# Expert gather of a two-layer diffusion backbone: groups of four slots in place of two, in the same ring of eight

## What is computed

```python
def peer(h, wq, keys, u_tab, v_tab):      # cut: N tokens, 8 heads, top 16 experts of each head
    q = (x @ wq).reshape(N, PEER_HEADS, 2, PEER_DKEY // 2)
    s = jnp.einsum('nhpd,hpkd->nhpk', q, keys)
    top_s, top_i = lax.top_k(s, K)
    ...
    def block(args):
        xb, eb, gb = args
        a = jax.nn.gelu(jnp.einsum('tkd,td->tk', u_tab[eb], xb), approximate=False)
        return jnp.einsum('tk,tkd->td', gb * a, v_tab[eb])
```

## Time and profile before

| | |
|---|---|
| time, median of 3 runs (lowest to highest) | 6070.39 us (6068.23 to 6082.94) |
| the profiled execution's own time | 6077.12 us |
| its span, first to last instruction | 6075.3 us |
| mean granted TensorE clock | 0.815 |
| busy: PE, VectorE, ScalarE, GpSimd | 4146.3, 2900.3, 1672.5, 1468.7 us |
| indirect gathers | 1342.26 MB, 55.1% of the 16 DMA engines over the span |
| other DMA | 361.79 MB, 16.2% |

### The profile page before, as it was taken

The page is one execution under the profiler, slowest core; times in us unless marked ns, Lnnn a source line. Parts: engine busy times, 40 slices in busy tenths (PEclk is TensorE's granted clock), DMA queues, the critical chain, the costliest instruction groups (busy, mean ns, idle before and its releaser), DMA issues.

```text
span 6075.3 us, 63558 instructions
## 1 busy us (share of the span) xinstructions
PE 4146.3 (68%) x22120; PEld 2508.5 (41%) x22120; DVE 2900.3 (48%) x6824; ACT 1672.5 (28%) x4712; POOL 1468.7 (24%) x1295
## 2 busy tenths in 40 slices
PE   3779668879894587547566666778847765556554
PEld 0567545556563344224223334567744432211111
DVE  1221657644446544664545443522184446754544
ACT  0210126333342343223322222310114422222222
POOL 0000012212221133223344341000003332335444
PEclk7769879968997798778788888957978877777777
DMA  8214448747895599679999995102439998889998
GB/s 337 93 52 140 169 169 306 291 164 274 312 381 228 204 410 398 264 280 367 366 401 418 392 421 206 42 1 100 159 124 388 420 370 320 331 338 421 410 415 363
DMA packets 258449, 1708.10 MB, mean 281 GB/s; under 512 B 37616, under 2 KB 39120, under 8 KB 71248
## 3 DMA queue, kind: packets, MB, share of 16 engines
q0 software_dynamic: 184320, 1342.26, 55.1%
q1 hardware_dynamic: 73808, 361.79, 16.2%
HBM read 1685.91 MB, written 17.92 MB: 280 GB/s over the span
## 4 chain that ended last, share of the span: by engine, by line
PE 42%; DMA 24%; DVE 14%; ACT 5%; issue 5%; DVEq 3%; POOL 3%; ACTq 2%; SPq 1%; PEld 0%; PEldq 0%; POOLq 0%
PE psum L398 25%; DMA arena<-in_uv,arena 21%; PE psum L722 10%; POOL arena L1026 3%; DVE arena L1858 3%; DVE arena L1775 1%; DVE arena L1768 1%; DVE arena L1769 1%; DMA arena<-in_w_ada 1%; PE psum L359 1%; PE psum L568 1%; PE psum L569 1%; ACT arena L1335 1%; ACT arena L1122 1%; DVE arena L1772 1%
## 5 line engine op out<-in xcount | busy, mean ns | idle before, releaser
L1026 POOL DMA_INDIRECT arena<-in_uv,arena x1280 | 1464.8, 1144 | 4571.3 <-PE psum L722 2919.2
L722 PE MATMUL psum<-arena 64*64 64x512 f32 x10240 | 1579.8, 748 | 1180.5 <-ACTq L1336 1101.5
L1858 DVE CUSTOM_DVE_ANT_0 arena<-arena 128x1024 f32<-128x1024 f32 x1280 | 1555.3, 1226 | 1412.1 <-DMA arena<-in_uv,arena 1359.2
L398 PE MATMUL psum<-arena 128*128 128x256 f32 x8352 | 1934.2, 391 | 101.2 <-DVEq L1355 80.1
L398 PEld LDWEIGHTS psum<-arena 128*128 128x128 f32 x8352 | 1604.4, 194 | 537.7 <-issue 174.8
L722 PEld LDWEIGHTS psum<-arena 64*64 64x64 f32 x10240 | 394.2, 158 | 2183.1 <-ACTq L1336 1502.1
L1329 ACT ACTIVATE arena<-arena 128x2 f32<-128x2 f32 x640 | 130.9, 204 | 1559.2 <-DVEq L1860 1543.2
L1335 ACT ACTIVATE arena<-arena 128x64 f32<-128x64 f32 x1280 | 375.9, 340 | 45.2 <-issue 1.0
L359 PE MATMUL psum<-arena 128*128 128x128 f32 (+1 forms) x680 | 131.0, 350 | 362.9 <-DVE arena L1410 115.0
L1332 ACT ACTIVATE arena<-arena 128x1 f32<-128x1 f32 x1280 | 307.4, 287 | 46.2 <-issue 2.4
L359 PEld LDWEIGHTS psum<-arena 128*128 128x128 f32 (+1 forms) x680 | 99.9, 183 | 414.2 <-issue 216.1
(11 more groups left out here) (201 smaller groups left out, 2712.3 us busy)
## 6 DMA issues: line engine op xcount, KB each, us to landing
arena<-in_w_mix SPq DMA_DIRECT2D x120, 768.0 KB, 7.5
arena<-in_w_in SPq DMA_DIRECT2D x88, 1024.0 KB, 5.7
arena<-in_w_ada SPq DMA_DIRECT2D x32, 1536.0 KB, 17.3
arena<-in_w_wq SPq DMA_DIRECT2D x40, 1152.0 KB, 5.4
arena<-in_w_wo SPq DMA_DIRECT2D x20, 1024.0 KB, 8.8
arena<-in_uv,arena POOLq DMA_INDIRECT x1280, 11.2
arena<-ada_rows SPq DMA_DIRECT2D x15, 512.0 KB, 5.2
arena<-x_rows SPq DMA_DIRECT2D x14, 512.0 KB, 6.2
```

The lines of the kernel that those rows point to most:

```text
L398: ins = mm(out, a, b, start=(i == 0), stop=(i == last))
L722: ins = mm(psum[o, r_ * 512:r_ * 512 + 512], DIAG[rows, c, :], RING[rows, sl, D + half * 512:D + (half + 1) * 512], start=first, stop=last ...
L1026: pool.indirect_dma_start(RING[:, sl, :], None, io["uv"], bass.IndirectOffsetOnAxis(IDX[:, t, h * TOPK + k:h * TOPK + k + 1], 0)).then_inc ...
L1858: V_.tensor_tensor_reduce(out=RING[:, sl, 0:D], in0=RING[:, sl, 0:D], in1=XT[:, u % 2, :], scale=1.0, scalar=0.0, op0=ALU.mult, op1=ALU.ad ...
```

## The change

Groups have four slots, so a unit has 32 groups and two groups share the ring of eight. The lags become 0, 1 and 2: ScalarE works, in call i, the group whose dots VectorE makes in the same call, and PE the group before. The leads become six groups (24 slots), and the two points in a unit at which SyncE loads the next tokens' activations and the residual are written as shares of `GROUPS`, which leaves them where they were. Nothing else is changed; each slot has the same instructions, except that there is one gelu, and one set of waits and signals, for four slots.

```diff
 RS = 8
-GS = 2
+GS = 4
 GROUPS = PH * TOPK // GS
-LAG_ACT, LAG_PE, LAG_TAIL = 1, 2, 3
+LAG_ACT, LAG_PE, LAG_TAIL = 0, 1, 2
...
-    return [(a, [], 0), (b, p0, 0), (c1, p1[:cut], 0), (c2, p1[cut:], 8), (d, [], 0), (e1, p2[:cut], 0),
-            ([("final", 2, ())], p2[cut:cut + GROUPS], 8), ([("final", 3, ())], p2[cut + GROUPS:cut + GROUPS + 16], 8),
-            ([("final", 4, ())], p2[cut + GROUPS + 16:], 16), ([("final", 5, ())], [], 0)]
+    return [(a, [], 0), (b, p0, 0), (c1, p1[:cut], 0), (c2, p1[cut:], 6), (d, [], 0), (e1, p2[:cut], 0),
+            ([("final", 2, ())], p2[cut:cut + GROUPS], 6), ([("final", 3, ())], p2[cut + GROUPS:cut + GROUPS + 16], 6),
+            ([("final", 4, ())], p2[cut + GROUPS + 16:], 6), ([("final", 5, ())], [], 0)]
...
-                    if g == 40 and u + 1 < len(UNITS) and state["xt"] == u + 1 and (UNITS[u + 1][0], UNITS[u + 1][1] // 2) in h2_ready:
+                    if g == GROUPS * 5 // 8 and u + 1 < len(UNITS) and state["xt"] == u + 1 and (UNITS[u + 1][0], UNITS[u + 1][1] // 2) in h2_ready:
...
-                    if g == 16:
+                    if g == GROUPS // 4:
```

## The result

The changed kernel takes 6627.05 us (median of 4 runs, 6619.59 to 6629.79) against 6070.22 us (median of 4 runs of the kernel before); the ratio is 1.0911, 95% interval 1.0892 to 1.0929. The profiled execution has a span of 6628.0 us. The forecast was 6563 us, range 6290 to 6800. The ratios further down are each against runs of the kernel before made beside the run in question.

The account below looks back on a forecast made before the run. Dense work bounds b and gathers at full DMA rate bound c2 and units 8 and 9; two groups lift the ring's loop above DMA time. Segment terms 161 + 136 + 40 + 86 + 25 + 25 + 20 = +493 gave 6563 us, range 6290 to 6800.

Parts of the forecast that it names:

- The loop: Ring of two groups of four, PE done to PE done: 25.5 us for eight slots, 408 us a unit.
- quick landing: Rival: four gathers landed after 13.0 us, loop 23.3 us, total 6406 us; chance 0.15.
- cold PE: Rival: all PE bursts at 1.2 GHz (7.4 us) and ScalarE's wait holding up dense work, total 6795 us; chance 0.13.
- some +200, 6270 us: Total by the skill page's DMA fit: four gathers landed some 11.6 us after first issue, loop 21.9 us.
- Units 8 and 9: Last gather-bound units: 408 us each against 333 and 322, +161 us (bounds +59 and +229).
- c2: Units 4 and 5, same loop with weight chunks: 424 us a unit against 360 and 352, +136 us.
- Route steps of e1: Eight steps of 12 slots, third group issued only after PE's burst: 10.8 us later each, +86 us.
- c1's route steps: Eight steps of eight slots, PE gets its second half group late: 3.1 us each, +25 us.
- merge steps: Steps with 110 + 160 slots and weight chunks: 3.35 us a slot against 3.2 before, +40 us (0 to +103).
- Small stages of c1: 88 slots with tight ScalarE-VectorE chains: +25 us (0 to 50), estimated from half of the rise a slot in c2.
- b: Segment where dense work sets the pace and covers the loop: +20 us (-20 to +60).
- Faster: Rival: DMA queue never runs dry; route steps gain 40 us, table loads in b some 20, total 6010 us; chance 0.04.

Follow-up runs that it names:

- two_act_in_step: Kernel before, groups of two, lags 0, 2, 3: ScalarE in step with the dots, PE two groups behind as before; 6094.2 us, ratio 1.0036.
- four_freed_singly: Changed kernel, but PE signals after every slot and GpSimd waits for one slot in place of four; 6288.57 us, ratio 1.0343 against the kernel before.
- two_in_step: Kernel before with groups of two kept and only the lags changed to 0, 1, 2; 6277.73 us, ratio 1.0333.
- two_ring_six: Kernel before with groups of two, lags 0, 1, 2 and a ring of six slots in place of eight; 6589.31 us, ratio 1.0839.
- one_pe_four: Kernel before with groups of one, lags 1, 4, 5 (PE four slots behind), eight bubbles, slots freed singly; 6031.58 us, ratio 0.9924.

## Why the prediction held

**The loop.** Predicted 25.5 us, measured 24.88 (25.4 the turn before). Term by term: first issue to fourth dot 15.2, measured 16.1 and 14.5; ScalarE 2.6, measured 2.4 (dot's end 6024.54 to 6026.94); PE 6.2, measured 6.53 and 6.04. The quick landing (13.0 us) was not seen in these units (the shortest of 64 is 13.2), the cold PE at 7.4 us neither (the longest burst is 6.6). The loop as cause is shown from two sides: groups of two with the same lags in calls bring units 8 and 9 back to 330 and 323 us, and an earlier release alone recovers 21 to 46 us a unit with groups of four.

The Trainium skill (DMA: Bandwidth & Descriptors, Anatomy of one DMA — SWDGE (gpsimd) path) would put the fourth landing some 11.6 us after the first issue, an estimate; in the trace the fourth dot starts after 14.5 and 16.1 us. The prediction did well to go by its rows. Its "some +200, 6270 us" for that fit is too low by its own steps: 21.9 us a loop gives +45 in units 8 and 9, +20 in c2, +57 in the e1 route steps and +110 for the rest, +232 and 6302 us.

**Units 8 and 9:** +161 predicted, +140 measured. **c2:** +136 predicted, +135 measured.

**Route steps of e1:** +10.8 us a step predicted, (359.5 - 299.2) / 7 = 8.6 measured. Timeline of one step of the changed kernel:

```profile
5557.16 1.23 DVE L1858 CUSTOM_DVE_ANT_0 arena<-arena 128x1024 f32<-128x1024 f32 x1 [0.16 <-issue]
...
5564.24 9.16 PE L722 MATMUL psum<-arena 64*64 64x512 f32 x64 [20.18 <-ACTq L1336]
...
5570.28 0.94 POOL L1026 DMA_INDIRECT arena<-in_uv,arena  x1 [21.24 <-PE psum L722]
...
5575.89 1.23 DVE L1858 CUSTOM_DVE_ANT_0 arena<-arena 128x1024 f32<-128x1024 f32 x1 [9.23 <-DMA arena<-in_uv,arena]
...
5584.20 1.23 DVE L1858 CUSTOM_DVE_ANT_0 arena<-arena 128x1024 f32<-128x1024 f32 x1 [1.26 <-DMA arena<-in_uv,arena]
...
5590.02 0.49 DVE L1765 MAX8 arena<-arena 128x8 f32<-128x128 f32 x2 [4.59 <-ACT arena L1299]
```

The order of events is the predicted one, counted from the first dot, with the prediction in brackets: PE at +7.1 (7.5), third group issued at +13.1 (14.0), fourth dot at +27.0 (29.2), VectorE's next head at +32.9 (35.1). The mis-sized term is the landing, 13.9 us here in place of 15.2. c1's route steps: 256.6 us for seven before, 276.2 after, 2.8 us a step where 3.1 was predicted.

**Mis-sized: the merge steps.** "Merge steps ... +40", while the 24 sigmoids (L1262) of the 30 steps span 294.5 us after in c1 against 251.3, and 401.3 against 346.4 in e1: +98 already. The term that was wrong is the price of before, "I take 3.2". Windows of these steps in c1, before, after, and with four slots freed singly:

```profile
2078.00:2329.00 251.00, 208.72 (x1173) 124.13 (x1173) 115.58 (x200) 118.50 (x269) 90.84 (x78) 0.94 0.98 396
```

```profile
2108.00:2402.00 294.00, 221.82 (x1185) 130.18 (x1183) 118.00 (x206) 106.77 (x254) 85.92 (x80) 0.86 0.89 349
```

```profile
2093.00:2356.00 263.00, 213.13 (x1186) 128.41 (x1184) 117.04 (x206) 107.59 (x256) 93.61 (x80) 0.92 0.98 395
```

Before, the DMA share is 0.98: merge steps were gather-bound too, at 3.06 us a slot in c1 and 2.89 in e1, close to the 2.93 that the prediction had worked out from the transfers alone. After, they take 3.51 and 3.34, near the predicted 3.35, and a median turn of 28.2 and 27.4 us where 26.8 was predicted (PE's burst is 5.3 and 5.1 us, not the warm 3.9). So the loop was right here too; what it replaced was cheaper than assumed.

The timeline of a c1 merge step after shows two waits that the sum did not hold:

```profile
2255.31 1.23 DVE L1858 CUSTOM_DVE_ANT_0 arena<-arena 128x1024 f32<-128x1024 f32 x1 [1.80 <-DMA arena<-in_uv,arena]
...
2260.30 0.38 ACT L1262 ACTIVATE arena<-psum 128x256 f32<-128x256 f32 x1
...
2260.71 0.42 DVE L1729 TENSOR_TENSOR arena<-arena,psum 128x256 f32<-128x256 f32 x1 [4.17 <-ACT arena L1262]
...
2261.31 1.23 DVE L1858 CUSTOM_DVE_ANT_0 arena<-arena 128x1024 f32<-128x1024 f32 x1 [0.17 <-issue]
...
2265.19 10.67 PE L398 MATMUL psum<-arena 128*128 128x256 f32 x48
...
2269.59 1.06 ACT L1335 ACTIVATE arena<-arena 128x64 f32<-128x64 f32 x4
...
2275.79 3.66 PE L722 MATMUL psum<-arena 64*64 64x512 f32 x32
```

From the last dot (ends 2256.54) it is 4.8 us to the next, spent in ScalarE's group, the sigmoid's table load, the sigmoid that waited behind them, and the product that needs it. And a diagonal ready at 2270.7 waits until 2275.79, since PE is in two dense steps. It is tempting to book the loss on these waits, but other runs speak against it. VectorE's product (L1729) in all waited for the 24 sigmoids of c1, before, after, and freed singly (us, times):

```profile
  DVE arena L1729: 27.6, 11
```

```profile
  DVE arena L1729: 111.2, 24
```

```profile
  DVE arena L1729: 107.4, 23
```

With single slots released the wait is still there, yet the same 24 sigmoids span 262.7 us, and 354.8 in e1: +20 in place of +98, at a DMA share of 0.98. In two_act_in_step it is 86.1 us for a span of 257.0. The wait for PE is not longer than before either: from the last diagonal of a group to PE's burst it is 25 us in all in c1 after, 68 before. So at least four fifths of what the 24 steps lost goes through the late release of slots, that is the loop; the waits show in VectorE's idle time and cost at most the rest.

**Small stages, b.** Small stages of c1: +25 predicted; from the last index write of c1 to the closing of unit 3 it is 288.6 us before and 321.6 after, +33. b: +20 predicted, -4 by closings. The closings flatter it: the last index write of b's routing stands at 2064.9 before and 2097.5 after, so b's dense end is 33 us later, and the table books that on unit 2. No run isolates what b lost.

**The sum.** Four terms were too high, by 42 us together (units 8 and 9, c2, the route steps of e1 and of c1). The merge steps were too low by some 70: with the six steps behind the sigmoids in c1 and in e1 they lost about 111 us, over the upper bound of 103. Small stages, b and ends of segments that no term held add some 30. So the total rose by 557 us where 493 was forecast, and a part of the agreement is luck: errors of both signs cancel. The bulk is not, since the loop gives the time a slot in all the gather-bound stages within some 5%.

**Rivals.** The gain that the rival *Faster* put in the route steps was not seen; there ScalarE alone in step costs 20 us with groups of two, and in b it gains 15 us. The loads of the gelu table fell by less than thought (25 of 140). The unchanged 5% of ScalarE in the chain fits that little hangs on them.

**What stays open.** four_freed_singly and two_in_step end within 11 us of each other (1.0343, 1.0333), but not by the same cause: the first keeps +26 and +24 us in units 8 and 9 and +29 and +22 in c2, the second -3 and +1, and +3 and +8; b's dense end is 19 us later in the first and 84 in the second. Nor does the 3.3% of two_in_step measure a part of the changed kernel's loss: PE one group behind is two slots behind with groups of two but four with groups of four, as in the kernel before. Half of the 209 us that four_freed_singly still costs stands in c2 and in units 8 and 9; in the latter its median turn is 21.6 us (19.9 before). How much of the other half comes from ScalarE in step with four slots and how much from coarse calls was not separated. The old lags with groups of four were not run: as the program is ordered, VectorE's call would wait for a gather that PE frees in the same call, behind dense work that needs VectorE.

## What to carry to other kernels

Count a ring in groups as well as in slots: gather time + dot + scale + matmul of one group is the least time for one turn, and it must stay under the transfer time of the whole ring; doubling the group at a fixed ring raises the first and leaves the second. Taking slots away lowers the second, as two_ring_six shows. A wait that is seen in a timeline is not yet a cost; look for a run that has the wait and not the loss. Grain of work and grain of release are separate choices, and releasing single slots alone took 9.1% of loss down to 3.4% here and gained 0.4% in the kernel before. Where engines run one program in order, the distance between producer and consumer, in slots, had an optimum here (four of two, four and six): too short, and the consumer's wait stands in front of its next dense step (seen in two_in_step's route step). Why too long costs was not isolated.

## What the runs showed that was not expected

- PE one group of two behind the dots costs 3.3%, and with ScalarE one call late as well (lags 1, 1, 2) 8.7%; units 8 and 9 do not show it at all (329 and 323 us).
- The landing of a burst of four varied with what else was queued: the fourth dot 13.9 us after the first issue in a route step, 14.5 and 16.1 in unit 8; for a pair 9.35 us on an idle DMA, and a median of 11.0 (12.4 in the turn shown) with a DMA share of 0.94 to 0.96.
- In one_pe_four PE is busy 217 us a unit at a granted clock of 0.65 for what takes 184 and 181 us at 0.74 and 0.76 in the kernel before, and the unit takes the same 322 to 332 us.
